# A top-2-of-8 expert layer on one core: four separate tests of an expert's count become a chain with alternatives, and an arm that has run jumps to the end of the loop

## The chip, the cores and the metric

The kernel runs on one core of one Trainium2 chip. The metric is device time in microseconds of one execution. One profiled execution of the kernel before is read here, beside the times of three other executions.

## The reference, cut to what matters

Two layers over 512 tokens of 1,024 features. The change lies in the channel mixer of layer 1, where each token goes to 2 of 8 experts, each a SwiGLU of width 3,584:

```python
def moe_swiglu(h, w_router, w1, w3, w2):
    logits = (h @ w_router).astype(jnp.float32)
    top_logit, top_e = lax.top_k(logits, TOP_K)
    gates = jax.nn.softmax(top_logit, axis=-1)
    ...
    counts = jnp.zeros((N_EXPERTS,), jnp.int32).at[e_flat].add(1)
    ...
    yb = lax.map(expert_block, (xb, block_e)).reshape(n_rows, D)
    y = jax.ops.segment_sum(yb * row_gate[:, None], row_tok, num_segments=T + 1)
```

with `swiglu(h, w1, w3, w2) = (silu(h @ w1) * (h @ w3)) @ w2`. How many tokens an expert gets is known only while the kernel runs.

## The kernel before

All matrix work is done to fp32 accuracy as three products of rounded high and low parts: `three` (L1851 to L1853) multiplies high by high, low by high and high by low. ScalarE rounds each unit of weights to its high part, VectorE subtracts to get the low part, SyncE's queue loads the next units. TensorE works through a program of its own in order and waits on semaphores.

The expert stage is a hardware loop over the 8 experts (`with t.loop(pe, NE, ...)`) whose body is `by_count`. It loads the expert's `kind`, a number that VectorE worked out from the token count: 0 for at most 128 tokens (one row tile), 1 for up to 32 more and 2 for up to 64 more (one row tile and a narrow piece of 32 or 64 rows), 3 for more than that (two row tiles). For each kind there is a separate copy of the program, an arm: `expert(tiles, r, more, m)`. An arm is a loop over 7 groups of hidden columns: `up_first` and `up_second` (with the narrow piece in `piece_up`, L2232), `turn_hidden` (L2278 to L2287) and `down` (piece in L2296). Its last group's `down` stands behind the loop, between `token_tiles` (L2222), which turn the next expert's tokens: three of the four before that `down`, the fourth after it. So the last matmuls of an expert are those of L2222, and the first of the next one is L1851 `ps<-hia,xth`. The line numbers L115 are those of the loop helper `Turns.loop`: its register arithmetic and its branches.

In the trace the arms can be told by their work: expert 0 takes arm 0, expert 1 arm 1 (products of L2232 in 32-row pieces), expert 2 arm 3, experts 3, 4 and 5 arm 0, expert 6 arm 2 and expert 7 arm 0.

The arms stand behind each other in TensorE's program in the order 0, 1, 2, 3. Each test is a compare-and-branch with its own line: L2350 ahead of arm 0, L2353 between arms 0 and 1, L2356 between 1 and 2, L2359 between 2 and 3. Behind arm 3 stand the end of the loop (L115) and the test for overflow rows (L2368). The other engines have no such tests: they run the same loop for every kind.

Of the kernel before, what the change touches and what calls it, by code (L numbers as in the profile page):

```python
# [34 lines left out]
NE = 8  # L35
# [11 lines left out]
PIECE = 32  # L47
PIECE_MAX = 64
# [77 lines left out]
def program(nc, small, xT_in, ctxT_in, rope, maskin, rconst, lnrow, w_mod, w_pre, w_moe, out):  # L126
    with ExitStack() as ctx:
# [1718 lines left out]
        def _(pe):  # L1846
            t = Turns()
# [396 lines left out]
            def up_first(tiles, r, m):  # L2244

                for j in (0, 1):
                    arrived(j)
                ks = [k for i in XT_ORDER for k in (2 * i, 2 * i + 1)]
                for s in range(tiles):
                    for i, k in enumerate(ks):  # L2250
                        if s == 0 and i % 2 == 0:
                            pe.wait_ge(xtl_ready, r * 4 - (3 - i // 2))
                        if m and i == KD - 1:
                            piece_up(0, m)
                        ins = up_part(0, tiles, s, i, k, i == 0, i == KD - 1)
                ins.then_inc(up_done[0], 1)
# [62 lines left out]
            def expert(tiles, r, more, m=0):  # L2319

                late = (("raw", WHERE[5][0]), "hl")
                for key in late:
                    t.skip(key, -1)
                with t.loop(pe, GROUPS, turn) as g:
                    up_first(tiles, r, m)
                    with pe.If(g > 0):
                        down(1, tiles, m)
                        turn_hidden(0, tiles, m)
                    up_second(tiles, g, m)
                    with pe.If(g < 1):  # L2330
                        pe.wait_ge(ys_a, r)
                        pe.wait_ge(ys_b, r)
                        for b in range(4 if m or tiles == 2 else 2):
                            pe.matmul(PS[:, 4 + b, 0:1], ident, BEFORE[:, 0:1], start=True, stop=True, skip_group_check=True)
                    down(0, tiles, m)
                    turn_hidden(1, tiles, m)
                if more is not None:
                    with pe.If(more):
                        pe.wait_ge(xg_in, r * 16 + 16)
                        for i in range(3):  # L2340
                            token_tiles(i)
                down(1, tiles, m).then_inc(y_full, 1)
                if more is not None:
                    with pe.If(more):
                        token_tiles(3)

            def by_count(e, r):
                kind = pe.value_load(RI[0:1, bass.ds(e, 1)], min_val=0, max_val=3)
                saved = dict(t.at)
                with pe.If(kind < 1):  # L2350
                    expert(1, r, e < NE - 1)
                t.at = dict(saved)
                with pe.If(kind == 1):  # L2353
                    expert(1, r, e < NE - 1, PIECE)
                t.at = dict(saved)
                with pe.If(kind == 2):  # L2356
                    expert(1, r, e < NE - 1, PIECE_MAX)
                t.at = dict(saved)
                with pe.If(kind > 2):  # L2359
                    expert(2, r, e < NE - 1)  # L2360

            pe.wait_ge(xg_in, 16)
            for i in range(4):
# [1 line left out]
            with t.loop(pe, NE, times(turn, GROUPS)) as e:  # L2365
                by_count(e, e + 1)
# [127 lines left out]
```

## Time and profile before

| | |
|---|---|
| median of 3 executions | 2247.52 us (2244.53 to 2247.78) |
| the profiled execution, its own time | 2246.7 us |
| its span in the trace | 2245.1 us |
| TensorE (PE) busy | 2146.2 us, 96% |
| VectorE (DVE) busy | 1493.3 us, 67% |
| ScalarE (ACT) busy | 1131.6 us, 50% |
| mean granted TensorE clock | 0.978 |

1.6 us of the profiled execution lie outside its span. PE is a matmul on TensorE, PEld a load of its weights, PEldq the sequencer that issues both: its branch and register instructions are not counted as busy, but their records with start and duration are in the trace. "issue" is time in which an engine waited for nothing that the profile shows. The DMA queue q8 carries instructions, not data.

### The profile page before, as it was taken

The numbers are of one execution on the slowest core, as the hardware profiler recorded it, in microseconds if no ns is written. First come the engines' busy times: TensorE is split into PE (matmuls) and PEld (weight loads), VectorE is DVE, ScalarE is ACT, GpSimd is POOL, SyncE is SP. The second block draws the span as 40 slices with busy tenths as digits, with TensorE's granted clock in tenths as the row PEclk, the third lists the DMA queues.
The fourth block names the chain that finished last, engine by engine and source line by source line (L and its number), as shares of the span: only waits on it lengthen the run. The fifth ranks groups of instructions, "written<-read, shape, count | busy, mean of one in ns | idle before, by whom it ended". The sixth has DMA issues, their size and how long they took to land.

```text
span 2245.1 us, 33136 instructions
## 1 busy us (share of the span) xinstructions
PE 2146.2 (96%) x12156; PEld 1715.7 (76%) x12157; DVE 1493.3 (67%) x1391; ACT 1131.6 (50%) x1278; POOL 368.8 (16%) x247
## 2 busy tenths in 40 slices
PE   6999999999999999799799999999999999999994
PEld 4876688887888888678677788888888887666882
DVE  3456656667457544789566645459999997555984
ACT  4135536222224522377555534347888885445872
POOL 0030004999991000100000000000000000000001
PEclk8999999999999999799899999999999999999997
DMA  8472022555443222399577755559999996557974
GB/s 328 195 293 83 1 97 100 188 189 200 168 179 120 76 93 102 142 375 371 197 275 271 306 197 184 193 183 410 367 395 378 384 370 251 211 218 269 380 292 158
DMA packets 78098, 515.87 MB, mean 230 GB/s; under 512 B 9008, under 2 KB 9264, under 8 KB 20944
## 3 DMA queue, kind: packets, MB, share of 16 engines
q1 hardware_dynamic: 61696, 442.85, 51.3%
q0 software_dynamic: 16336, 72.11, 8.5%
q8 instruction: 46, 0.75, 0.1%
q14 instruction: 20, 0.16, 0.0%
HBM read 482.41 MB, written 32.51 MB: 229 GB/s over the span
## 4 chain that ended last, share of the span: by engine, by line
PE 88%; DVE 6%; issue 2%; ACT 1%; DMA 1%; SPq 0%; POOL 0%; DVEq 0%; ACTq 0%; POOLq 0%
PE ps L1851 25%; PE ps L1853 24%; PE ps L1852 24%; PE ps L2232 3%; PE ps L2296 2%; PE ps L603 2%; PE ps L558 2%; PE ps L614 2%; PE ps L2278 1%; DVE lo L1191 1%; PE ps L1910 1%; PE ps L562 1%; DVE fl L1495 1%; DMA raw_pair<-w_mod 1%; PE ps L2029 0%
## 5 line engine op out<-in xcount | busy, mean ns | idle before, releaser
L1851 PE MATMUL ps<-ah,hi 128*128 128x512 f32 (+1 forms) x768 | 286.8, 373 | 5.7 <-DVE al L1356 2.4
L1853 PE MATMUL ps<-ah,lo 128*128 128x512 f32 (+1 forms) x768 | 284.9, 371 | 0.0
L1852 PE MATMUL ps<-al,hi 128*128 128x512 f32 (+1 forms) x768 | 284.9, 371 | 0.0
L1439 DVE TENSOR_TENSOR lo<-raw,hi 128x2048 fp32r<-128x2048 f32 x112 | 255.8, 2284 | 0.0
L1439 DVE TENSOR_TENSOR loa<-raw_pair,hia 128x2048 fp32r<-128x2048 f32 x112 | 251.1, 2283 | 1.1 <-ACT hia L960 1.1
L1439 DVE TENSOR_TENSOR lob<-raw_pair,hib 128x2048 fp32r<-128x2048 f32 x112 | 251.7, 2283 | 0.0
L960 ACT ACTIVATE hia<-raw_pair 128x2048 fp32r<-128x2048 f32 x112 | 214.4, 1915 | 49.9 <-DMA raw_pair<-w_moe 49.8
L1191 DVE TENSOR_TENSOR lo<-raw_pair,hi 128x2048 fp32r<-128x2048 f32 x59 | 183.8, 3118 | 80.0 <-ACT hi L848 78.5
L960 ACT ACTIVATE hi<-raw 128x2048 fp32r<-128x2048 f32 x112 | 214.8, 1918 | 11.1 <-DMA raw<-w_moe 11.1
L1851 PE MATMUL ps<-hia,xth 128*128 128x512 f32 x504 | 204.2, 405 | 16.2 <-issue 14.6
L960 ACT ACTIVATE hib<-raw_pair 128x2048 fp32r<-128x2048 f32 x112 | 215.0, 1921 | 1.0 <-DMA raw_pair<-w_moe 0.9
L1087 ACT ACTIVATE se<-ps 128x512 f32<-128x512 f32 x112 | 66.9, 598 | 274.6 <-PE ps L1853 274.6
L1719 DVE TENSOR_TENSOR he<-se,ps 128x512 f32<-128x512 f32 x112 | 77.0, 687 | 192.2 <-ACT se L1087 191.8
L1851 PE MATMUL ps<-hi,hh 128*128 128x512 f32 x504 | 200.8, 399 | 2.9 <-DVE hl L1723 2.9
L1851 PE MATMUL ps<-hib,xth 128*128 128x512 f32 x504 | 202.4, 402 | 0.0
L811 POOL DMA_DIRECT2D expert_y<-ys x8 | 5.8, 724 | 1169.0 <-DVE ys L1737 1059.2
L1853 PE MATMUL ps<-hia,xtl 128*128 128x512 f32 x504 | 197.4, 392 | 0.0
L1852 PE MATMUL ps<-loa,xth 128*128 128x512 f32 x504 | 197.0, 391 | 0.0
L1853 PE MATMUL ps<-hib,xtl 128*128 128x512 f32 x504 | 196.9, 391 | 0.0
L1853 PE MATMUL ps<-hi,hl 128*128 128x512 f32 x504 | 196.7, 390 | 0.0
L1852 PE MATMUL ps<-lo,hh 128*128 128x512 f32 x504 | 196.6, 390 | 0.0
L1852 PE MATMUL ps<-lob,xth 128*128 128x512 f32 x504 | 196.4, 390 | 0.0
(309 smaller groups left out, 4050.0 us busy)
## 6 DMA issues: line engine op xcount, KB each, us to landing
raw_pair<-w_moe SPq DMA_DIRECT2D x224, 1024.0 KB, 6.7
raw<-w_moe SPq DMA_DIRECT2D x112, 1024.0 KB, 6.8
raw_pair<-w_pre SPq DMA_DIRECT2D x59, 1024.0 KB, 4.8
raw_pair<-w_mod SPq DMA_DIRECT2D x20, 1024.0 KB, 7.2
raw_pair<-w_mod POOLq DMA_DIRECT2D x14, 1024.0 KB, 5.2
rawm<-w_mod POOLq DMA_DIRECT2D x14, 1024.0 KB, 5.5
dispatched_x<-zt POOLq DMA_DIRECT2D x22, 512.0 KB, 10.8
xg<-dispatched_x POOLq DMA_DIRECT2D x8, 1024.0 KB, 11.3
```

What stands on the lines that cost most here:

```text
L558: return pe.matmul(PSF[:, at:at + BLK * n], Q[rows_, j, b * BLK:(b + 1) * BLK], keys[rows_], start=True, stop=True, skip_group_check=True)
L603: ins = pe.transpose(PSF[:, 3072 + (i - a) * BLK:3072 + (i - a + 1) * BLK], PR[2 * (p % 2) + f][:, c * BLK:(c + 1) * BLK], ident)
L614: ins = pe.matmul(PS[HD * f:HD * f + HD, 7, (p % 2) * BLK:(p % 2 + 1) * BLK], v, PTS[p % 2][:, n * f + c, :], start=(c == 0), stop=(c == n ...
L960: act.activation(HI_OF[j], raw8(r), ACT.Copy).then_inc(hi_ready[h], 1)
L1087: act.activation(SE[:], up_view(q, 0), ACT.Silu).then_inc(se_ready, 1)
L1191: dve.tensor_tensor(LO[h][:], RAW[r][:], HI[h][:].bitcast(F32), ALU.subtract).then_inc(raw_used[r], 1)
L1439: dve.tensor_tensor(LO_OF[j], raw8(r), HI_OF[j].bitcast(F32), ALU.subtract).then_inc(raw_used[r], 1)
L1719: dve.tensor_tensor(HE[:], SE[:], up_view(q, 1), ALU.mult).then_inc(he_ready, 1)
L1851: pe.matmul(outp, wh, ah, start=first, stop=False, skip_group_check=True)
L1852: pe.matmul(outp, wh, al, start=False, stop=False, skip_group_check=True)
L1853: return pe.matmul(outp, wl, ah, start=False, stop=last, skip_group_check=True)
L2232: ins = pe.matmul(outs[m * j:m * (j + 1), :, 0:wide], XTF[:, k, 0:m], RAWU[q][:, :, k, wide * j:wide * (j + 1)], start=(k == 0), stop=(k = ...
```

## The change

Tests two, three and four are put into the Else branch of the one before. The arm's own code is the same.

```diff
                 saved = dict(t.at)
                 with pe.If(kind < 1):
                     expert(1, r, e < NE - 1)
-                t.at = dict(saved)
-                with pe.If(kind == 1):
-                    expert(1, r, e < NE - 1, PIECE)
-                t.at = dict(saved)
-                with pe.If(kind == 2):
-                    expert(1, r, e < NE - 1, PIECE_MAX)
-                t.at = dict(saved)
-                with pe.If(kind > 2):
-                    expert(2, r, e < NE - 1)
+                with pe.Else():
+                    t.at = dict(saved)
+                    with pe.If(kind < 2):
+                        expert(1, r, e < NE - 1, PIECE)
+                    with pe.Else():
+                        t.at = dict(saved)
+                        with pe.If(kind < 3):
+                            expert(1, r, e < NE - 1, PIECE_MAX)
+                        with pe.Else():
+                            t.at = dict(saved)
+                            expert(2, r, e < NE - 1)
```

Before, an arm that has run goes on to the next test, fails it, jumps over the next arm to the next test, and so on to the end of the loop. Now its last instruction branches to the end of the loop. On the way to its arm an expert passes the same tests as before, but for arm 3, which needs no fourth one. The two branches of L2344 end an arm in both kernels (one for `more`, one for the last expert): their target was the next test and is now the loop's end. The order of instructions changes on TensorE alone.

On TensorE, where arm 0 ends and arm 1 begins (rows of `ps<-small,xg` are the last token tiles of the arm, L115 opens the loop over groups of the next arm):

```order
 L2222 MATMUL ps<-small,xg 128x128 x4
 L2344 UNCONDITIONAL_BRANCH
-L2353 COMPARE_AND_BRANCH
+L2354 COMPARE_AND_BRANCH
 L115 UNCONDITIONAL_BRANCH
 L115 ISA
```

The test keeps its place and gets a new line number; it is now reached only from L2350, and L2344 branches past it.

On TensorE, where arm 2 ends and arm 3 begins:

```order
 L2222 MATMUL ps<-small,xg 128x128 x4
 L2344 UNCONDITIONAL_BRANCH
-L2359 COMPARE_AND_BRANCH
 L115 UNCONDITIONAL_BRANCH
 L115 ISA
```

The fourth test is gone, so everything from arm 3 on stands one instruction earlier. Between arms 1 and 2 test L2356 becomes L2358 in its place.

## Rows read from the trace of the kernel before

**Rows 1.** The page: busy time by engine; the queue that fetches instructions.

```profile
PE 2146.2 (96%) x12156; PEld 1715.7 (76%) x12157; DVE 1493.3 (67%) x1391; ACT 1131.6 (50%) x1278; POOL 368.8 (16%) x247
...
q8 instruction: 46, 0.75, 0.1%
```

**Rows 2.** Windows: gap, experts 1, 2 and 3; each number as its header says.

```profile
core 0: us, PE busy (x) PEld busy (x) DVE busy (x) ACT busy (x) POOL busy (x), PEclk, DMA share, GB/s
...
1079.30:1091.90 12.60, 0.02 (x1) 0.03 (x1) 4.59 (x4) 3.44 (x4) 4.57 (x8) 0.58 0.36 120
...
1095.00:1265.80 170.80, 170.67 (x1725) 129.28 (x1724) 111.33 (x72) 96.16 (x89) 0.00 (x0) 1.00 0.69 272
1265.80:1504.20 238.40, 238.13 (x1090) 197.33 (x1089) 115.44 (x75) 98.55 (x93) 4.55 (x8) 1.00 0.54 200
1504.20:1626.30 122.10, 121.06 (x556) 99.22 (x554) 114.39 (x75) 98.31 (x93) 4.55 (x8) 1.00 0.97 380
```

**Rows 3.** Waits of PE, 950 to 2200 us: total, times, longest.

```profile
PE ps L1851 <- issue: 14.6, 6, 12.7
```

**Rows 4.** Timeline of PE where expert 0 ends: start, duration.

```profile
1078.63 0.60 PE L2222 MATMUL ps<-small,xg 128*128 128x128 f32 x4
1091.88 0.79 PE L1851 MATMUL ps<-hia,xth 128*128 128x512 f32 x1 [12.65 <-issue]
...
1094.96 0.40 PE L1852 MATMUL ps<-loa,xth 128*128 128x512 f32 x1
1095.19 0.40 PE L1853 MATMUL ps<-hia,xtl 128*128 128x512 f32 x1
```

**Rows 5.** Timelines: DVE at 1080 us; first weight load of expert 2.

```profile
1080.06 0.69 DVE L1730 TENSOR_TENSOR xtl<-ps,xth 128x512 fp32r<-128x512 f32 x1 [0.19 <-ACT xtf L1100]
...
1265.84 0.19 PEld L1851 LDWEIGHTS ps<-hia,xth 128*128 128x128 f32 x1
```

**Rows 6.** Sequencer branch records, 1075 to 1095: min/median/max ns, first and last start.

```profile
L2344 PEldq COMPARE_BRANCH  x1: 65/65/65, 1075.8 to 1075.8; - x1
L2353 PEldq COMPARE_BRANCH  x2: 71/2132/4193, 1076.0 to 1091.2; - x2
L2356 PEldq COMPARE_BRANCH  x1: 4960/4960/4960, 1080.2 to 1080.2; - x1
L2359 PEldq COMPARE_BRANCH  x1: 4401/4401/4401, 1085.3 to 1085.3; - x1
```

**Rows 7.** The same where expert 1 ends, 1258 to 1266 us.

```profile
L2356 PEldq COMPARE_BRANCH  x2: 200/206/213, 1262.6 to 1264.9; - x2
L2359 PEldq COMPARE_BRANCH  x2: 77/144/210, 1262.9 to 1265.1; - x2
```

**Rows 8.** DMA: 1075.9–1080.2, 1080.2–1085.2, 1085.2–1089.7, 1089.7–1092, 1092–2196.4.

```profile
q8 instruction: 2, 0.03, 3.6%
...
q8 instruction: 2, 0.03, 4.0%
...
q8 instruction: 1, 0.02, 1.7%
...
q8 instruction: 1, 0.02, 2.5%
...
DMA packets 46224, 318.00 MB, mean 288 GB/s; under 512 B 5392, under 2 KB 5392, under 8 KB 9232
```

**Rows 9.** Up to 21.4 us, where the first q8 packet starts.

```profile
0.00:21.40 21.40, 11.24 (x104) 4.44 (x105) 1.41 (x6) 3.00 (x6) 0.20 (x4) 0.96 0.92 373
```

**Rows 10.** The only record of the test behind the loop.

```profile
L2368 PEldq COMPARE_BRANCH  x1: 3357/3357/3357, 2196.4 to 2196.4; - x1
```

**Rows 11.** DMA packets, 1264 to 1269 us.

```profile
DMA packets 266, 1.93 MB, mean 385 GB/s; under 512 B 31, under 2 KB 31, under 8 KB 31
```

**Rows 12.** A gap of 2.96 us and the clock behind it.

```profile
2200.35 3.43 PE L2378 MATMUL ps<-dg,small 128*128 128x128 f32 x16 [2.96 <-DVE dg L1798]
...
2200.80:2204.20 3.40, 2.98 (x15) 2.68 (x13) 0.00 (x0) 2.36 (x8) 0.00 (x0) 0.50 1.00 358
```

## The prediction

> **What bounds the kernel now.** I read the profile's page first. TensorE is busy 2146.2 of 2245.1 us [rows 1], so an edit to its program counts only where it stands idle. The windows, one per expert, show that it hardly does: 170.67 of 170.80 us in expert 1, 238.13 of 238.40 in expert 2, and even in an expert of arm 0, where the DMA share is 0.97, 121.06 of 122.10 [rows 2]. The exception is one window of 12.60 us at the end of expert 0, with 0.02 us of matmul in it [rows 2]. The waits give 14.6 us of "issue" ahead of L1851 over the whole expert stage, and 12.7 of them are this one gap [rows 3]. The timeline places it: the last token tiles (L2222) start at 1078.63 for 0.60 us, the first product of expert 1 at 1091.88 [rows 4]. The data isn't what is late: the last low part of the tokens ends at 1080.06 + 0.69 = 1080.75 [rows 5].
>
> The sequencer's own records explain the gap. Behind L2344 at 1075.8 come three tests, and they take 4.193, 4.960 and 4.401 us, from 1076.0 to 1089.7 [rows 6]. At the end of expert 1 the same tests take 0.200 to 0.213 us when they jump, 0.077 when they don't [rows 7]. So what costs is not the branch but the first jump to a place. The queue that brings instructions shows what happens: 2 packets during the first test, 2 in the second, 1 in the third, 1 behind it, and none in the 1104 us after 1092 [rows 8]. There are 46 such packets in all, 0.75 MB [rows 1], and the built program has 11,769 TensorE instructions, when a product of fp32r or a transpose counts as 2 (weights and matmul) and an fp32 product as 4, as their records do. That is 256 a packet, a page from here on.
>
> **Where the pages lie.** Counting positions in the program of before: loop head 9,443, arm 0 9,448, test L2353 9,700, arm 1 9,701, L2356 10,337, arm 2 10,338, L2359 10,780, arm 3 10,781, end of loop 11,221, and 11,667 where L2368 jumps to. The first packet comes at 21.4 us, when 104 to 105 weight loads have been issued [rows 9]; that is about position 216, where the sequencer enters page 1. So page k begins near 256k - 40. I read the rule "on entering a page, the next one is fetched; a jump to a page that isn't there waits for it" off the packets: arm 0 lies in page 37 and ends in page 38 (from 9,688). L2353 sits in 38: fetch 39 as next, then 40 as target (2 packets). L2356 is in 40: next 41, target L2359 in 42 (2 packets). L2359: next is 43, and the target 11,221 is in 43 too (1 packet). Then 44 as next (1 packet). Six packets, each accounted for, and after that pages 37 to 44 are all held, eight of them, so nothing is fetched for 1104 us.
>
> **The change, part by part.**
>
> (1) *End of expert 0.* Arm 0 now branches from page 38 straight to 11,220 in page 43. One wait takes the place of three. Its price: the first one's 4.193 us [rows 6], since here too page 39 is fetched ahead of the target. The wait starts where L2353's did, 1076.0, so the sequencer is at the loop's end at 1080.2 instead of 1089.7. What follows (loop branch, load of `kind`, tests, semaphores) is the same code; so the first product moves from 1091.88 by 4.96 + 4.40 + two small steps between records of 0.06, together 9.48, to 1082.40. That is later than the tokens' 1080.75, and TensorE is still the last to be ready. The gap is then 3.2 us and not 12.65. **Gain 9.5 us.** Bounds: 10.3 at L2368's 3.357 [rows 10], if page 39 is not in the way; 8.7 if the wait is as dear as L2356's 4.960.
>
> (2) *End of expert 1, a new wait.* Pages 41 and 42 came in before because the chain of tests ran through them. Now, after expert 0, the core holds 37 to 39, 43 and 44. Arm 1 (9,701 to 10,336) runs into 39 and 40 in a straight line, so 40 and 41 come as next pages while it works. Page 42, where arm 3 begins, isn't touched. Expert 2 takes arm 3: L2358 jumps from page 40 to 42 and waits. Before, L2356 was at 1264.9 for the second time [rows 7]; two tests at the arm's end fall away (0.21 us each and a step of 0.06), so L2358 starts at 1264.3. Its price lies between 3.357 us, the one wait with a single fetch and a quiet memory [rows 10], and 4.960 [rows 6]. The nearest is L2359's 4.401, a single fetch with store traffic beside it; here the loads run at 385 GB/s [rows 11], so I take 4.6. Ready at 1268.9, plus the 0.6 from test to first product that the end of expert 0 shows (1091.2 to 1091.88), gives 1269.5 for the first weight load, which was at 1265.84 [rows 5]. **Loss 3.7 us** (2.4 to 4.0; 5 if the loads hold the packet up by another microsecond). Who waits for it: everything behind in TensorE's order, and as it is the bound through experts 2 to 7 [rows 2] nothing gives the time back.
>
> (3) *The granted clock.* After the 12.65 us gap the clock was at its lower level: from 1091.88 seven products take 3.08 us to 1094.96, then one takes 0.23 [rows 4]; 7 x 0.23 is 1.61, so the gap cost another 1.5. [...] The two gaps of the new kernel are about 3.2 and 3.4 us, so I expect some of it behind each: about 1.1 behind the first (0.4 less than before) and 1.2 behind the second (bounds 0 and 1.7). **Loss 0.8 us net** (bounds: gain 1.5, loss 1.9).
>
> (4) *The other ends.* At the ends of experts 2 to 6 up to three jumps of 0.27 us each fall away. The covered tests ran while TensorE still had products queued, as the loads that follow without a pause show at 1265.84 [rows 5]. Worth nothing; uncovered they would be 3 us in all (10 jumps). Expert 6 takes arm 2, in pages 40 to 42: all there by then. L2368's wait for page 45 stays, and TensorE waits for VectorE behind it [rows 12].
>
> Sum: -9.5 + 3.7 + 0.8 = -5.0 us, from the profiled execution's own 2246.7 to 2241.7. That execution is 0.8 us below the median of the three, so against that median I expect about 2242: 0.22% less. 0.2%, 4.5 us, is about what a measurement of this kernel tells from no change, and this forecast lies just beyond it.
>
> [...] The records show a wait at the first jump to each of three places [rows 6] and 0.2 us for the same jumps at the end of expert 1, over up to two pages [rows 7], and no fetch in 1104 us of such jumps [rows 8]. [...]
>
> **The rivals.**
>
> A: *the deferred wait doesn't come or is hidden.* Page 42 would have to be there by the end of expert 1, say because more than one page ahead is fetched in a straight line. For it: arm 1 has 170 us to do so. Against: each step of rows 8 is used up by one next page. Time: -9.5 - 0.4 = -9.9, 2236.8.
>
> B: *the jump back isn't free any more (ends slower).* Before, the eight pages were always one stretch without a hole. If they must be, the jump from 38 to 43 throws 37 to 39 away, and each end of an expert pays for the jump out (L2344) and the jump back (L115). Price: two waits of 4.2 less about 1 us of cover (the sequencer needs all of 1262.6 to 1265.84 at such an end today, and would lose tests), 7.4 us at six ends, 44; at expert 0 the second wait takes 4.2 of the 9.5 back. Time: 2246.7 - 5.3 + 44 = 2285. It decides as soon as the jump back waits at expert 0 and at one end more (-5.0 + 4.2 + 7.4 = +6.6). Against: the jump from 38 to 40 left page 37 in place, since L115 went back to it with no packet of its own [rows 8]. For it: nothing in this trace has a hole. [...]
>
> C: *the new wait is dearer than I take it, or the saving smaller,* with the loads' traffic in the way (6 us at L2358) and the lower clock whole behind both gaps: -9 + 5.2 + 2.0 = -1.8, 2244.9. There is no wait over 4.96 in rows 6, but the DMA share was 0.36 in that window [rows 2], not full.
>
> **How the numbers follow.** The forecast (two waits where three were, at about 4.2 and 4.6) gets 0.76; within it the clock and the two prices spread -3.2 to -7.2, and two thirds of that lie beyond -4.5. A gets 0.08, C 0.09, B 0.07. Faster by over 0.2%: 0.51 + 0.08 = 0.59. Within 0.2%: 0.25 + 0.09 = 0.34. Slower: 0.07. The range runs from 2237.5, which leaves out half of A, to 2245.5, which takes in C.
>
> **What the changed profile would show.** Step 1: 4.2 us between L2344's record at 1075.8 and L115's, a first product at 1082.4, and three q8 packets between 1076 and 1083. Step 2: one record of L2358 of 4 to 5 us at about 1255 (1264.3 less 9.5), with one q8 packet, and a gap of some 3.4 us ahead of expert 2; two more packets while arm 1 runs. Step 3: a clock of 0.50 behind each gap. Step 4: no long record at the end of experts 2 to 6. Still 46 packets in all: none is saved, only moved under work. More than 46, or a long L115, would be rival B; no long L2358 would be A. The sum is wrong if the cover isn't where I think: if expert 2's gap is well over 4 us, or if arm 1's straight run stalls at page 40.

## The result and the profile after

The changed kernel takes **2250.09 us** (median of 19 runs, 2248.31 to 2253.08) where the kernel before takes 2245.30 in the same session (19 runs, 2242.34 to 2249.33). The ratio is 1.0021, with a 95% interval of 1.0014 to 1.0028: slower by 3 to 6 us, where 5 us less were forecast. The profiled execution took 2249.01 us, its span is 2247.4.

The page of the changed kernel; its two rows answer to [rows 1]. There are six more instruction packets (52) than before (46).

```profile
PE 2148.7 (96%) x12156; PEld 1716.8 (76%) x12157; DVE 1492.4 (66%) x1391; ACT 1131.7 (50%) x1278; POOL 368.8 (16%) x247
...
q8 instruction: 52, 0.85, 0.2%
```

The timeline of TensorE in the changed kernel, where expert 0, expert 1 and expert 2 end (start, duration, line, tiles; in brackets the idle time before). It answers to [rows 4] and [rows 5].

```profile
1074.43 0.60 PE L2222 MATMUL ps<-small,xg 128*128 128x128 f32 x4
1078.61 0.79 PE L1851 MATMUL ps<-hia,xth 128*128 128x512 f32 x1 [3.58 <-issue]
...
1255.41 0.60 PE L2222 MATMUL ps<-small,xg 128*128 128x128 f32 x4
1267.34 0.79 PE L1851 MATMUL ps<-hia,xth 128*128 128x512 f32 x1 [11.33 <-issue]
...
1507.74 0.48 PE L1851 MATMUL ps<-hia,xth 128*128 128x512 f32 x1
```

The gap at the end of expert 0 is 3.58 us and not 12.65: the first step of the forecast came. But the end of expert 1, where TensorE ran on without a pause, now has a gap of 11.33 us. The waits of TensorE from 950 to 2200 us (total, times, longest) show the exchange; the first row answers to [rows 3], and the lower two are waits for VectorE, of which more below.

```profile
PE ps L1851 <- issue: 16.9, 7, 11.3
...
PE ps L2278 <- DVE he L1719: 2.6, 6, 1.0
...
PE ps L2296 <- DVE hl L1723: 1.0, 2, 0.7
```

The windows of the changed kernel: the gap, the start of expert 1, the rest of it, the second gap, the start of expert 2, the rest of it. They answer to [rows 2].

```profile
core 0: us, PE busy (x) PEld busy (x) DVE busy (x) ACT busy (x) POOL busy (x), PEclk, DMA share, GB/s
1074.70:1078.20 3.50, 0.33 (x3) 0.09 (x1) 3.31 (x4) 3.14 (x4) 0.00 (x0) 0.83 0.02 5
1078.20:1086.00 7.80, 7.39 (x21) 5.63 (x21) 1.68 (x1) 0.34 (x1) 3.83 (x7) 0.64 0.53 185
1086.00:1255.80 169.80, 167.87 (x1712) 126.83 (x1711) 111.31 (x72) 96.32 (x89) 0.74 (x1) 1.00 0.70 275
1255.80:1267.30 11.50, 0.21 (x2) 0.00 (x0) 4.02 (x3) 3.48 (x4) 3.82 (x7) 0.74 1.01 389
1267.30:1278.00 10.70, 10.66 (x38) 8.66 (x39) 0.00 (x0) 0.00 (x0) 0.73 (x1) 0.80 0.46 162
```

From the last token tile of expert 0 to the first product of expert 3 the kernel before takes 425.6 us (1078.63 in [rows 4] to 1504.27) and the changed one 433.3 (1074.43 to 1507.74). The 7.7 us between them, piece by piece:

| piece | before | after | difference |
|---|---|---|---|
| last token tile of expert 0 to first product of expert 1 | 13.25 | 4.18 | -9.1 |
| expert 1, without the gap behind it | 173.96 | 177.40 | +3.4 |
| gap ahead of expert 2 | 0 | 11.33 | +11.3 |
| expert 2 | 238.43 | 240.40 | +2.0 |

The clock and the waits for VectorE are in the second and fourth row: behind each gap a stretch of products at the lower level (granted clock 0.64 and 0.80 in the windows), and 0.71 + 0.96 us of waits in expert 1. The first products at the upper level again are these two, behind the first and the second gap:

```profile
1083.86 0.40 PE L1851 MATMUL ps<-hia,xth 128*128 128x512 f32 x1
...
1271.67 0.39 PE L1852 MATMUL ps<-loa,xth 128*128 128x512 f32 x1
```

The sequencer's branch records of the changed kernel (min/median/max ns of one, first and last start), end of expert 0, end of expert 1, and the tests behind it. They answer to [rows 6] and [rows 7].

```profile
L2344 PEldq COMPARE_BRANCH  x2: 65/2310/4555, 1071.6 to 1071.7; - x2
...
L2344 PEldq COMPARE_BRANCH  x2: 65/3086/6106, 1251.7 to 1252.6; - x2
...
L2358 PEldq COMPARE_BRANCH  x1: 6162/6162/6162, 1260.6 to 1260.6; - x1
```

Of each pair of L2344 the short one is the test whether more experts follow, the long one the jump out of the arm. At the end of expert 0 the jump takes 4.56 us in place of three tests of 4.2 to 5.0. At the end of expert 1 there are **two** waits, of 6.1 and 6.2 us: the test ahead of arm 3, which was foreseen, and the jump out of arm 1 to the loop's end, which was not: it goes to the same place as the jump of expert 0, 180 us earlier.

The queue that brings instructions, in the changed kernel from 1071 to 1078, 1089 to 1103, 1252 to 1259, 1259 to 1268, 1862 to 1900 and 2070 to 2090 us (packets, MB, share of the DMA engines), answering to [rows 8].

```profile
q8 instruction: 3, 0.05, 4.2%
...
q8 instruction: 2, 0.03, 0.9%
...
q8 instruction: 1, 0.02, 0.9%
...
q8 instruction: 2, 0.03, 1.4%
...
q8 instruction: 2, 0.03, 0.3%
...
q8 instruction: 2, 0.03, 0.6%
```

What the traces show of pages is this. The size: in the kernel before, from its first packet at 21.48 us to the 22nd at 388.94, TensorE has 2,640 products and 2,637 weight loads on record, 251 to a packet where the forecast took 256, with branches and register instructions not counted. The time: a packet takes 0.9 to 2.5 us, and TensorE doesn't stop for one that comes in a straight run: the two inside arm 1, at 1090.83 and 1102.12, lie in a stretch (1086 to 1255 us) whose only waits are for VectorE, 1.0 and 0.7 us. So what comes in a straight run is taken to be the page after the one being run. **The trace doesn't say which page a packet brings.** Every page number here is the author's estimate, from positions counted in the built program and from the times of packets and waits.

Read so, the three packets at the jump of expert 0 (1072.27, 1072.74 and 1077.06 us) are page 39 as next, page 43 as target and page 44 as next, and the two inside arm 1 are 40 and 41. If all these stayed, only page 42 and what comes next to it would be missing at the end of expert 1. But the jump out of arm 1 goes to the place where the jump of expert 0 had gone, and it waits again, for 6.11 us where it was 4.56 the first time; one packet comes in during its wait (1256.31), two more behind it (1261.89 and 1264.46). That the code at this place was no longer held is what the second wait shows; that it is page 43, and that the two packets in between were 40 and 41, is the reading. Four more packets come in expert 6, under queued products: no gap there. Twelve in the expert stage, where there were six: that is the difference of 52 and 46. (Outside the stage 39 or 40 packets come in, by execution, in all kernels here without hints or a shift, so totals can differ by one.)

**The theory to test** (theory 1 in the expectations): what TensorE's instruction memory holds depends on the order of first visits. If pages are fetched in ascending order, all stay; if a jump goes past pages that were never fetched, its target is put where the next pages in line are put later. **Rivals:** the branch that ends an arm is dear in itself when it goes far (two pages and more); any far jump is dear while loads fill the memory (389 GB/s in the gap ahead of expert 2); a page that isn't used for over 100 us is lost.

### The profile page after: what moved, and what is told of

It reads as the page before. It is cut to its first block, busy times and chain, and to the rows that moved or that the text cites. A ratio compares the mean times of both kernels' runs of the same rounds, so it can differ in the third digit from the quotient of the medians.

```text
span 2247.4 us, 33123 instructions
## 1 busy us (share of the span) xinstructions
PE 2148.7 (96%) x12156; PEld 1716.8 (76%) x12157; DVE 1492.4 (66%) x1391; ACT 1131.7 (50%) x1278; POOL 368.8 (16%) x247
## 4 chain that ended last, share of the span: by engine, by line
PE 88%; DVE 6%; issue 2%; DMA 2%; ACT 2%; SPq 0%; DVEq 0%; POOL 0%; ACTq 0%; POOLq 0%
PE ps L1851 25%; PE ps L1853 24%; PE ps L1852 24%; PE ps L2232 3%; PE ps L2296 2%; PE ps L603 2%; PE ps L614 2%; PE ps L558 2%; PE ps L2278 1%; DVE lo L1191 1%; PE ps L1910 1%; DVE fl L1495 1%; PE ps L562 1%; DVE loa L1439 1%; DMA raw_pair<-w_mod 1%
## 5 line engine op out<-in xcount | busy, mean ns | idle before, releaser
L1851 PE MATMUL ps<-ah,hi 128*128 128x512 f32 (+1 forms) x768 | 286.1, 373 | 5.7 <-DVE al L1356 2.4
L1851 PE MATMUL ps<-hia,xth 128*128 128x512 f32 x504 | 205.4, 407 | 18.6 <-issue 16.9
L1851 PE MATMUL ps<-hi,hh 128*128 128x512 f32 x504 | 200.9, 399 | 2.9 <-DVE hl L1723 2.9
L1851 PE MATMUL ps<-hib,xth 128*128 128x512 f32 x504 | 202.3, 401 | 0.0
```

What stands on the lines that cost most here:

```text
L1851: pe.matmul(outp, wh, ah, start=first, stop=False, skip_group_check=True)
```

## The experiments

Each kernel was timed five rounds or more beside the kernel before on the same chip. Where a ratio is given, it is to that kernel, with its 95% interval.

**arm0_jumps.** Only arm 0 jumps to the end; arms 1 to 3 keep the kernel before's tests.

```diff
                 with pe.If(kind < 1):
                     expert(1, r, e < NE - 1)
-                t.at = dict(saved)
-                with pe.If(kind == 1):
-                    expert(1, r, e < NE - 1, PIECE)
+                with pe.Else():
+                    t.at = dict(saved)
+                    with pe.If(kind == 1):
+                        expert(1, r, e < NE - 1, PIECE)
...
```

> Arm 0 alone jumps to the end of the loop; arms 1 to 3 keep the three tests of the kernel before. Theory 1 (pages lost): the jump past pages 39 to 42 leaves pages 43 and 44 where arm 1's straight run then puts 40 and 41, so that page 43 is gone at the end of expert 1 and page 42 was never brought. Then one wait of 4.2 to 4.6 us at the end of expert 0 (gap 3.3 to 3.6 us where it was 12.65), and at the end of expert 1 one or two waits of some 6 us and a gap of 5 to 12 us; 2246 to 2251 us, and over 46 instruction packets. Theory 2 (the branch of arm 1 itself, over a distance of two pages and more, is what costs 6.1 us while the loads fill the memory): arm 1 no longer has that branch, only page 42 is late, a gap of at most 5.5 us, 2243 us.

Measured: 2251.4 us, 1.0027 (1.0018 to 1.0036). The tests in the region of expert 1's end, and the first product of expert 2:

```profile
L2357 PEldq COMPARE_BRANCH  x2: 207/2996/5785, 1254.0 to 1267.4; - x2
L2360 PEldq COMPARE_BRANCH  x2: 77/2804/5530, 1259.9 to 1267.7; - x2
```

```profile
1268.34 0.79 PE L1851 MATMUL ps<-hia,xth 128*128 128x512 f32 x1 [10.86 <-issue]
```

The first test waits 5.8 us, for page 42 by the positions, where arm 3 begins, and the second 5.5 us, for page 43. Arm 1 has no jump of its own here, and the gap is the same. Arm 0's jump past pages 39 to 42 is enough for the whole loss. Three packets come with the two waits (1257.47, 1263.10 and 1270.11 us), by the positions 42, 43 and 44, in ascending order, and in expert 6 no packet comes in, where the changed kernel, which fetched 43 ahead of 42, has four. That too speaks for the order, as far as the reading of the packets holds.

**arm1_jumps.** The other half: arm 0 goes through the tests, arms 1 and 2 jump to the end.

```diff
                 with pe.If(kind < 1):
                     expert(1, r, e < NE - 1)
                 t.at = dict(saved)
                 with pe.If(kind == 1):
                     expert(1, r, e < NE - 1, PIECE)
-                t.at = dict(saved)
-                with pe.If(kind == 2):
-                    expert(1, r, e < NE - 1, PIECE_MAX)
+                with pe.Else():
+                    t.at = dict(saved)
+                    with pe.If(kind == 2):
+                        expert(1, r, e < NE - 1, PIECE_MAX)
+                    with pe.Else():
...
```

> The other half: arm 0 goes through the tests as in the kernel before, and arms 1 and 2 jump to the end of the loop. Theory 1 (pages lost): every page is visited first in ascending order, so all of 37 to 44 stay; three waits at the end of expert 0 with 12.6 us of gap, none at the end of expert 1, 46 packets, and a time within 0.1% of the kernel before (2245.3). Theory 2 (the branch of arm 1 is dear by itself under full load): 6 us at L2344's branch at the end of expert 1, some 3 to 5 us of them as a gap, 2249 us.

Measured: 2245.36 us, 0.9992 (0.9983 to 1.0001). The jump out of arm 1, over the same distance and beside traffic of 422 GB/s (1257.8 to 1261.0 us), and the waits of TensorE from 950 to 2200 us:

```profile
L2344 PEldq COMPARE_BRANCH  x2: 65/117/169, 1257.8 to 1258.7; - x2
```

```profile
PE ps L1851 <- issue: 14.9, 6, 13.0
```

The jump takes 0.17 us, where the changed kernel's takes 6.11 at the same place beside 420 GB/s. So neither the distance nor the traffic is dear by itself. No packet comes at this jump, and one does at the dear one: what differs is whether the code there is held.

**arm3_second.** The changed kernel's chain, with the arms in the order 0, 3, 1, 2.

```diff
                 with pe.Else():
                     t.at = dict(saved)
-                    with pe.If(kind < 2):
-                        expert(1, r, e < NE - 1, PIECE)
+                    with pe.If(kind > 2):
+                        expert(2, r, e < NE - 1)
                     with pe.Else():
                         t.at = dict(saved)
-                        with pe.If(kind < 3):
-                            expert(1, r, e < NE - 1, PIECE_MAX)
+                        with pe.If(kind < 2):
+                            expert(1, r, e < NE - 1, PIECE)
...
```

> The chain of the changed kernel with its arms in another order in the program: arm 0, arm 3, arm 1, arm 2. Arm 1 now lies behind arm 3, so that its straight run at expert 1 goes into the last pages ahead of the loop's end, and arm 3 begins in page 38, next to arm 0. Theory 1 (pages lost): one wait of 4.2 to 4.6 us at the end of expert 0; one for arm 1's first page at the start of expert 1 right behind it, since the jump to the loop's end went past it (about 4.2 us more: gap 7 to 8 us), or none if that page is the one fetched as next; at the end of expert 1 no gap. 2236 to 2242 us. Theory 2 (a jump over several pages under full load waits whatever came before): 6 us at the branch of arm 1 or at the test ahead of arm 3 at the end of expert 1, 2245 us or more.

Measured: 2242.74 us, 0.9984 (0.9975 to 0.9993), faster than the kernel before. The jumps out of arm 0 and arm 1, and the waits of TensorE:

```profile
L2344 PEldq COMPARE_BRANCH  x2: 65/2000/3935, 1071.0 to 1071.2; - x2
...
L2344 PEldq COMPARE_BRANCH  x2: 65/2050/4036, 1252.5 to 1253.5; - x2
```

```profile
PE ps L1851 <- issue: 8.2, 7, 3.4
```

The first theory's "no gap" at the end of expert 1 was wrong: there is one of 2.89 us, and the time lies just above its range. Arm 1 runs in a straight line from page 39 to the first 66 instructions of page 42. The jump to page 43 waits 4.0 us and not 6.1, which would fit a fetch of 43 as next page that began when the sequencer entered 42, just ahead of the jump; the trace doesn't show whose packet it is (there are two, at 1255.17 and 1260.83 us). Part of what the smaller gaps save is given back in expert 1: one wait of 2.04 us for `hl` from VectorE, which is late behind ScalarE's `hia`, which waited for its weights. In the profile nothing is left of the saving: from the last token tile of expert 0 to the first product of expert 3 this kernel takes 426.0 us, the kernel before 425.6. So the 0.16% of the timed runs is measured, but its place is not shown.

**walk_once.** Arm 0 goes through the tests at expert 0 alone and jumps to the end at experts 3, 4, 5 and 7.

```diff
                 with pe.If(kind < 1):
                     expert(1, r, e < NE - 1)
-                t.at = dict(saved)
-                with pe.If(kind == 1):
+                with pe.If(kind * 8 - e > -1):
+                    t.at = dict(saved)
+                    with pe.If(kind == 1):
...
```

> Arm 0 goes through the three tests at expert 0 only (all of the kernel before's first visits in their ascending order) and jumps to the end of the loop at experts 3, 4 and 5; arms 1 to 3 as in the kernel before. The loop is some 30 instructions longer, its end lies where page 44 begins. Theory 1 (pages lost when first visits are out of order): three waits at expert 0 as before, none at the end of expert 1; as fast as the kernel before within 0.1%, if the loop still fits what is held; if it doesn't, packets on every turn and a gap of 3 us or more at several ends, 2255 us or more. Theory 2 (far jumps are dear under load): waits of some 6 us at the ends of experts 3 to 5, which have loads at the full rate in part.

Measured: 2246.96 us, 1.0002 (0.9993 to 1.0010). Its waits of TensorE and its instruction packets:

```profile
PE ps L1851 <- issue: 14.9, 6, 12.8
...
q8 instruction: 46, 0.75, 0.1%
```

One ascending walk at expert 0 is enough: afterwards arm 0's jumps to the end, over five pages, take 0.21 us at most (L2352), and no packet comes in from 1087 to 2193 us. Nothing is lost in the 100 us and more between visits (arm 2, with page 41 by the positions, first runs in expert 6, 780 us after the walk, and waits for nothing). That takes away the third rival. The loop is 2 instructions longer than before, not 30; its last one is number 11,224, where page 44 begins by the estimate of 256k - 40, and it still fits (46 packets). The estimate isn't good to a single instruction.

**before_shift.** The kernel before with 24 instructions more ahead of the loop (waits that are already met), nothing else.

```diff
+            for _ in range(48):
+                pe.wait_ge(tr_free, 4)
             pe.wait_ge(xr_ready, 1)
             pe.wait_ge(routed, 1)
```

(Two such waits become one instruction.)

> The kernel before, with 24 instructions (waits that are met already) ahead of the expert loop and nothing else: the loop then lies at positions 9467 to 11246 and its last instructions are in page 44, not 43. Theory 1 (eight pages are held, and entering a page fetches the next one): each turn enters page 44 and so fetches 45, over page 37, where the loop begins; every turn after the first then waits for page 37 and for more behind it: at least 2 packets and one wait of 4 to 6 us per turn, 20 to 60 us in all, 2265 to 2305 us and 60 packets or more. Rival (more than eight pages are held, or the next page isn't fetched so early): 46 packets and 2245 to 2247 us.

Measured: **2368.28 us, 1.0542** (1.0528 to 1.0555), 123 us more for a shift of 24 instructions. Packets, the waits of TensorE from 950 to 2330 us, and the records between expert 1 and expert 2:

```profile
q8 instruction: 100, 1.64, 0.4%
...
PE ps L1851 <- issue: 121.9, 11, 31.3
```

```profile
L2361 PEldq COMPARE_BRANCH  x2: 77/3406/6735, 1279.7 to 1308.1; - x2
L115 PEldq COMPARE_BRANCH  x1: 7115/7115/7115, 1286.6 to 1286.6; - x1
L2352 PEldq COMPARE_BRANCH  x1: 2709/2709/2709, 1294.5 to 1294.5; - x1
L2355 PEldq COMPARE_BRANCH  x1: 5460/5460/5460, 1297.3 to 1297.3; - x1
L2358 PEldq COMPARE_BRANCH  x2: 5138/5392/5647, 1274.0 to 1302.8; - x2
```

By the estimate of 256k - 40, the loop of the kernel before begins in page 37 and its last instruction is number 11,222, just ahead of page 44: seven pages, and an eighth that is fetched as next. Shifted by 24, it ends in page 44 and would need 45 as next, a ninth. The six packets of the walk at expert 0 are followed by none for 1104 us in the first kernel and by more at seven of the eight ends in the second, 100 in all. Six waits of 2.7 to 7.1 us follow each other in one gap of 31.3. Of the 123 us, 107 are longer waits ahead of L1851 (121.9 where there were 14.6). It is twice the upper end of what I had expected; that each refetch goes over a page that is wanted soon is the likely reason, not one that a run isolates. Room for eight pages is an estimate from these two kernels. That the page fetched longest ago goes first doesn't agree with the changed kernel: between the two waits at the loop's end, 4.56 and 6.11 us, only three packets came, by the reading 44, 40 and 41, and not eight.

**walk_first.** The version that this points to: the kernel before with one more turn of the expert loop, ahead of expert 0, in which no test succeeds (`kind` is 4). It runs while TensorE waits for the first tokens, and fetches all pages in ascending order. The zeroing products (L2334 of the kernel before) are in bf16, which saves 28 positions, and 23 instructions ahead of the loop put its head at the start of page 37 (9,434) and its last instruction at 11,219, five ahead of page 44. The waits for the first tokens and the load of `kind` move into the loop with it.

```diff
-            with t.loop(pe, NE, times(turn, GROUPS)) as e:
-                by_count(e, e + 1)
+            with pe.Fori(0, NE + 1) as i:
+                e = pe.snap(e_reg, min_val=0, max_val=NE - 1)
...
+                by_count(e, e + 1)
...
+                with pe.If(i < 1):
+                    pe.wait_ge(xr_ready, 1)
+                    pe.wait_ge(routed, 1)
+                    pe.wait_ge(xg_in, 16)
+                    for q in range(4):
+                        token_tiles(q)
+                pe.reg_mov(e_reg, i)
+                pe.reg_load(kind_reg, RI[0:1, bass.ds(i, 1)])
```

> The kernel before with its four separate tests, and a turn of the expert loop ahead of expert 0 in which no test succeeds, run while TensorE waits 12.6 us for the first tokens: the sequencer walks through all pages of the loop in ascending order while it has nothing else to do. Instructions that do the same with fewer positions (the products that zero a column of psum in bf16 instead of fp32) keep the loop within seven pages. If the pages are a ring filled in order of first visit (theory 1), six packets move ahead of expert 0 (935 to 950 us), there is no long test at the end of expert 0 and none at the end of expert 1: gaps of about 1 us or less where there were 12.65, 10 us less idle time, part of it given back because weights for expert 1 then come too late; 2236 to 2240 us. If instead a page that isn't used for over 100 us is lost (rival), the waits at the end of expert 0 come again and the time is 2245 or more.

Measured: **2235.87 us, 0.9958** (0.9945 to 0.9971); once more, as walk_first_again:

> The same kernel as walk_first, on the chip of the other three, so that the chain can be compared with it: 2236 us again, 0.3 to 0.5% under the kernel before.

Measured: 2235.58 us, 0.9944 (0.9930 to 0.9958). The three tests of the empty turn in walk_first, its longest wait of TensorE, and the window of the two ends of experts 0 and 1:

```profile
L2351 PEldq COMPARE_BRANCH  x1: 4852/4852/4852, 942.7 to 942.7; - x1
L2354 PEldq COMPARE_BRANCH  x1: 6062/6062/6062, 947.6 to 947.6; - x1
L2357 PEldq COMPARE_BRANCH  x1: 5381/5381/5381, 953.7 to 953.7; - x1
```

```profile
PE ps L2220 <- issue: 19.7, 1, 19.7
```

```profile
1050.00:1285.00 235.00, 233.23 (x2014) 180.09 (x2013) 164.66 (x109) 141.62 (x135) 9.12 (x16) 1.00 0.74 287
```

In that window TensorE works 233.2 us of 235 (221.9 in the kernel before, same window), and its clock stays at the upper level. The waits are the same ones as at the end of expert 0, only earlier, and not wholly hidden: the walk takes some 18 us, a test of 2.2 us ahead of the three included, and the gap ahead of the first token tiles grows from 12.6 to 19.7 us. Other transfers run beside the three tests (DMA share 0.24, 0.41 and 0.93), but their times don't follow the share. A walk that starts 7 us earlier wasn't tried.

**zero_bf16.** The kernel before with nothing but the shorter zeroing products.

```diff
-pe.matmul(PS[:, 4 + b, 0:1], ident, BEFORE[:, 0:1], start=True, stop=True, skip_group_check=True)
+pe.matmul(PS[:, 4 + b, 0:1], ident.bitcast(mybir.dt.bfloat16)[:, 0:P], BEFORE[:].bitcast(mybir.dt.bfloat16)[:, 0:1], start=True, stop=True, skip_group_check=True)
```

> The kernel before with the products that zero a column of psum in bf16 and nothing else, which walk_first needs to stay within seven pages. 14 products in the text of the four arms, 2 or 4 executed per expert, 0.12 us of each saved at most: 24 executed, 0 to 3 us. If what walk_first gains is the walk, this one is at most 2 us faster than the kernel before (2243 to 2246); if it is the shorter products, it is at 2237.

Measured: 2243.99 us, 0.9989 (0.9980 to 0.9998), on the chip of walk_first_again (2235.58). So 8.4 of the 10 us are the walk, with the moved waits and load that it needs.

**walk_chain.** walk_first with the changed kernel's chain, and a fourth test (`kind < 4`) ahead of arm 3.

> The empty turn of the loop ahead of expert 0, as in walk_first, but with the four tests as the changed kernel's chain (a fourth test ahead of arm 3, so that the empty turn passes all of them). If pages lost or never brought are all that makes the change slow, none of its long jumps is left: 45 packets, no gap over 1.7 us between expert 0 and expert 7, and the time of walk_first within 0.1% (2236), since the jumps that the chain saves lie under queued products. If the chain's jump out of an arm is dear of itself: 2240 us or more.

Measured: 2236.41 us, 0.9957 (0.9943 to 0.9971), beside 0.9944 (0.9930 to 0.9958) of the four separate tests: no difference that these runs can tell. There is no wait over 1.6 us ahead of L1851 left, and the window from 1050 to 1285 us has 233.2 us of products as in walk_first. With the pages there, the chain costs nothing and saves nothing that these runs can tell.

**after_hint and arm3_hint.** The changed kernel's order, and the order 0, 3, 1, 2, with an instruction behind the group loop of arms 0, 1 and 2 that tells the sequencer the target of the jump at the arm's end. The chain is written with explicit branches, and the zeroing products of the last arm are in bf16 to keep the loop within page 43. `hint=at` lets `expert` mark the place behind its group loop.

```diff
+                pe.br_eq(kind_reg, 0, on_true="by_count_arm0", on_false="by_count_test1")
+                with nc.body("by_count_arm0", valid_engines=[mybir.EngineType.PE]):
+                    at = []
+                    expert(1, r, e < NE - 1, hint=at)
+                    pe.br("by_count_done").branch_hint(at[0])
...
```

> The changed kernel's chain with a branch prefetch hint behind the group loop of arms 0, 1 and 2 for the jump that ends the arm (some 12 to 15 products ahead of it), and the zeroing products of arm 3 in bf16 so that the loop keeps within seven pages. If the hint fetches the target's page ahead: L2344's wait at the end of expert 0 falls from 4.6 us to 0.3 to 2 us, and the one at the end of expert 1 from 6.1 to 1 to 4, while the test ahead of arm 3 still waits 6 us for page 42; gap of 6 to 8 us ahead of expert 2, 2240 to 2245 us. If the hint does nothing on this chip: as the changed kernel, 2250 us.

> The order arm 0, arm 3, arm 1, arm 2 with the same hints. If the hint fetches ahead: the two remaining waits (3.9 us at the end of expert 0, 4.0 us at the end of expert 1, gaps of 3.4 and 2.9 us) shrink to 1 us or less each, part of it given back to weights that come later than TensorE would take them; 2236 to 2240 us. If it does nothing: as without hints, 2242.7.

Measured: after_hint 2243.20 us, 0.9990 (0.9980 to 1.0001); arm3_hint 2245.88 us, 1.0013 (0.9999 to 1.0027), with runs from 2237.9 to 2259.2. The three long records of after_hint: the jumps out of arm 0 and arm 1, and the test ahead of arm 3.

```profile
L2361 PEldq COMPARE_BRANCH  x1: 2278/2278/2278, 1071.9 to 1071.9; - x1
L2368 PEldq COMPARE_BRANCH  x1: 3549/3549/3549, 1246.9 to 1246.9; - x1
L2371 PEldq COMPARE_BRANCH  x1: 5907/5907/5907, 1252.0 to 1252.0; - x1
```

With the hint the jump waits 2.3 us where it waited 4.6, and 3.5 where it waited 6.1, as if its fetch began ahead of it; the test ahead of arm 3, for which there is no hint, costs 5.9 us where it cost 6.2. The gap ahead of expert 1 is 1.2 us and the one ahead of expert 2 8.2 (3.6 and 11.3 in the changed kernel), and by the ratios to the kernel before this version is some 7 us faster than the changed kernel. The explicit branches and the bf16 products came in with the hint; no run takes them apart, but the two shorter waits show the hint's part. In the other order the median is 3 us worse than without hints (on another chip), and the spread four times as wide, though the profiled execution was a good one (span 2236.3). In its profile the jump out of arm 1 has no long record any more and no gap behind it. But at the end of expert 0 there are now two waits, the jump out of arm 0 and the test that jumps over arm 3, and the gap is 5.05 us where it was 3.41 without hints; the forecast of 1 us or less was wrong there:

```profile
L2361 PEldq COMPARE_BRANCH  x1: 2490/2490/2490, 1071.6 to 1071.6; - x1
...
L2364 PEldq COMPARE_BRANCH  x1: 3540/3540/3540, 1075.6 to 1075.6; - x1
```

What makes its longer executions long (up to 2259.2) is not settled; none of them was profiled.

**after_again.** The changed kernel a second time.

> The changed kernel once more, for a second profile of the two gaps: 3 to 4 us ahead of expert 1 and 10 to 12 us ahead of expert 2 if what is fetched depends on the order of the code alone; other gaps if it depends on what else the memory does at the time. 2250 us.

Measured: 2250.83 us, 1.0021 (1.0011 to 1.0030). Its gaps are 3.08 and 10.62 us, its three waits 4.06, 5.61 and 5.94, and again twelve packets come in during the expert stage. Both executions wait at the same three places. How much each wait costs differs by up to 0.5 us between them. The second packet inside arm 1 comes at 1124.34 us and not at 1102.12, some 22 us later, so "next page on entering a page" isn't exact as to when; nothing waits for it in either.

## Why the prediction was wrong

**Step (1), the end of expert 0, was right.** One wait in place of three: 4.56 us where 4.19 was taken, gap 3.58 where 3.2 was forecast, gain 9.1 where 9.5. The second profile has 4.06 and 3.08. It needs a correction that the forecast didn't have: the stage behind it can't use the whole gain. Expert 1 has two waits for VectorE of 0.71 and 0.96 us that the kernel before has not at the same products (L2296 and L2278). The timeline of the changed kernel shows the first of them:

```profile
1095.30 1.92 ACT L960 ACTIVATE hia<-raw_pair 128x2048 fp32r<-128x2048 f32 x1 [5.79 <-DMA raw_pair<-w_moe]
1097.12 0.58 ACT L1091 ACTIVATE hh<-ps 128x512 fp32r<-128x512 f32 x1
...
1097.90 0.69 DVE L1723 TENSOR_TENSOR hl<-ps,hh 128x512 fp32r<-128x512 f32 x1 [5.46 <-ACT hf L1092]
...
1098.65 1.07 PE L2296 MATMUL ps<-raw,hf 128*32 128x256 f32 x16 [0.71 <-DVE hl L1723]
```

ScalarE's `hia` waits 5.8 us for its weights until 1095.3, `hh` and then `hl` come behind it, and L2296 waits for `hl`. In the kernel before the same `hl` ends at 1108.61 and L2296 starts at 1110.10, 1.5 us later, without a wait. So some 1.7 us were given back, since the loads don't come earlier because TensorE does.

**Step (2), the end of expert 1, is the step that failed.** It said that after expert 0 "the core holds 37 to 39, 43 and 44", and that 40 and 41 would come to these as next pages while arm 1 works. Two packets came in, as forecast, but the code at the loop's end, page 43 by the positions, was no longer there afterwards: the jump to it waited 6.1 us. arm0_jumps has the same loss without any jump out of arm 1; arm1_jumps has the jump without the loss; walk_chain has the whole chain without the loss once the tests were walked through in order. Instead of one wait of 4.6 us there were two of 6.1 and 6.2, a loss of 11.3 where 3.7 was forecast. About 6 us of that is the second wait, and 1.6 the price of a wait: I had taken it from [rows 6] with a bound of 4.96, where the DMA share was 0.04, 0.30 and 0.65 in the three tests, while the loads here run at full share (1.01 in the window of the gap). The two waits there are 5.5 to 6.0 us in after_again and arm0_jumps. Traffic isn't all of the price: the jump at the end of expert 0, with next to none beside it, takes 4.56 us, more than the third test's 4.40 at 0.65. Its window (the last three numbers are granted clock, DMA share and GB/s):

```profile
1071.70:1076.30 4.60, 3.33 (x16) 2.52 (x16) 4.41 (x5) 4.08 (x8) 0.00 (x0) 1.00 0.05 7
```

**Step (3), the granted clock, had the right sign and too small a size.** 0.8 us net was forecast, 1.1 behind the first gap and 1.2 behind the second in place of the 1.5 of before. Counted as the forecast counted them, twelve products behind the first gap take 5.25 us (1078.61 to 1083.86) where 12 x 0.23 is 2.76, so it cost 2.5; ten behind the second take 4.33 (1267.34 to 1271.67), so it cost 2.0. That is 3.0 us net. The 1.1 and 1.2 us that the forecast took for the two gaps are shown by no run. A shorter gap did not bring back the clock, and the length of the gap doesn't say what it costs: behind gaps of 12.65, 12.8, 13.0 and 13.1 us (the kernel before, walk_once, arm1_jumps, zero_bf16) seven, six, fourteen and seven products are slow, in 3.1, 2.7, 6.1 and 3.1 us; behind the 1.23 us of after_hint the granted clock is 1.00.

**Step (4), the other ends: right in the time.** No gap at the ends of experts 2 to 6. But "all there by then" was wrong for the pages of arm 2: four packets come in expert 6 (1873.40 to 2078.18 us), under queued products and without a gap.

**The packets.** "Still 46 packets in all" was wrong, 52, and by its own words "more than 46 would be rival B". Rival B came nearest, in that a hole in the stretch of pages costs something, but it had the wrong victim: I let it throw away 37 to 39, from which came a wait at each jump back and 2285 us. No record of L115, the jump back, is over 0.26 us in the stage (0.252 at most). What was lost lies ahead, at the loop's end, and only at the end of expert 1 does TensorE wait for it. Rival C (a dearer wait) is part of the answer: 6.2 us at L2358 were its 6. No case held two waits at the end of expert 1 alone.

The sum by the steps: -9.1 for the first gap, +11.3 for the second, +3.0 for the clock and +1.7 for VectorE's waits give +6.9 of the table's 7.7; 0.7 us of expert 1 has no row. The timed runs say 4.8 (3.1 to 6.3). The stage takes 432.8 to 433.3 us in three profiles with arm 0's jump (after, after_again, arm0_jumps) and 425.4 to 427.4 in four where expert 0 walks through the tests (before, walk_once, arm1_jumps, zero_bf16): 5.4 to 7.9 us apart. What remains between that and the timed 4.8 is open; it is no more than single profiles differ by ahead of the stage (the last token tile of expert 0 is at 1078.63 before and at 1074.43 after, with the same code up to there).

**What stays open:** where exactly a target page is put, and so which page goes. The order of events is shown (a wait of 4.56 us at the loop's end with its packets, two packets in arm 1, a wait of 6.11 us at the same place with another packet); the pages' numbers are an estimate, and their places in the memory are not shown.

## What to carry to other kernels

When a loop with several arms is longer than a page or two, list where each test, arm and end lies in pages and in which order they are first visited; a chain of tests that looks like waste may be what fills the instruction memory in order, as in the kernel before (2245.3 us, 2250.1 without it). Take a page as 256 instructions and room for eight of them, one for the next, as an estimate from walk_once (46 packets) and before_shift (100 packets): the step from fitting to not fitting cost 123 us here, more than the 9.1 us that leaving out the tests saved at expert 0. If waits for instructions can't be avoided, put the first walk through the code where the engine waits for data anyway (8.4 us gained in walk_first_again beside zero_bf16).

## What the runs showed of the hardware

- In the kernels without hints or a shift TensorE's sequencer waits 3.3 to 3.7 us at a jump that brings packets behind the expert loop, 3.9 to 5.0 at the end of expert 0 (DMA share 0.04 to 0.65 in the kernel before), and 5.5 to 6.2 at the end of expert 1, where the DMA share is 0.95 to 1.03 (352 to 421 GB/s); only arm3_second has 4.0 there. A jump that meets no packet takes 0.17 us (arm1_jumps, L2344) to 0.39 us (changed kernel, expert 6), over up to five pages of 256 instructions.
- In a loop that fits, where TensorE waits depends on the order of the first visits: at the end of expert 1 the same chain of jumps has waits of 6.1 and 6.2 us (changed kernel) or none (walk_chain, where TensorE's longest wait ahead of L1851 from 960 to 2180 us is 0.4 us).
- A straight run showed no wait for instructions in the expert stage of any of the 14 traces (in the changed kernel two packets come inside one, at 1090.83 and 1102.12 us): every idle time of TensorE over 0.5 us there lies at a jump or is a wait for VectorE.
- 24 instructions ahead of the loop, which do nothing, made this kernel 5.4% slower (before_shift, 2368.28 us, 100 packets for 46).
- A branch hint 12 products and the token tiles ahead took 2.3 to 2.6 us off such a wait in a profile (after_hint, 2.28 us for 4.56 and 3.55 for 6.11), but the timed runs don't gain dependably.
- Behind gaps of 12.65 to 13.1 us TensorE works at the lower level (granted clock 0.50) for 2.7 to 6.1 us, and behind one of 3.58 us for 5.3 us.
